# The third head group of a dilated attention: 32 by 32 score products, probabilities turned by VectorE, values re-ordered by DMA

## What is computed

```python
def dilated_window_group(q, k, v, window, dilation):
    span = window // dilation            # 128 in every group
    L = S // dilation                    # 512, 128, 32 tokens of one residue class
    # tokens are gathered by residue class mod dilation; in each class query t
    # attends the keys j <= t of its class, at most span back
    scores = einsum('bdhnqe,bdhnke->bdhnqk', qb, kw) * D ** -0.5
    m = max(scores); p = exp(scores - m); l = sum(p)
    out = einsum('bdhnqk,bdhnke->bdhnqe', p, vw) / l
    lse = m + log(l)
# the groups' outputs are weighed by softmax(lse) over the groups, then @ w_out
```

## Time and profile before

| | us |
|---|---|
| median of 3 runs (lowest, highest) | 2112.24 (2111.99, 2112.79) |
| the profiled execution, its own time | 2111.53 |
| its span, first to last instruction | 2109.7 |
| PE busy | 2098.6 |
| DVE, ACT, POOL busy | 999.5, 743.0, 1138.0 |
| attention's V1 and V2 | about 824 to 879 of the span |

### The profile page before, as it was taken

The page is one execution under the profiler, slowest core; times in us unless marked ns, Lnnn a source line. Parts: engine busy times, 40 slices in busy tenths (PEclk is TensorE's granted clock), DMA queues, the critical chain, the costliest instruction groups (busy, mean ns, idle before and its releaser), DMA issues.

```text
span 2109.7 us, 28007 instructions
## 1 busy us (share of the span) xinstructions
PE 2098.6 (99%) x11130; PEld 1743.3 (83%) x11130; DVE 999.5 (47%) x1144; ACT 743.0 (35%) x862; POOL 1138.0 (54%) x816
## 2 busy tenths in 40 slices
PE   9999999999999999999999999999999999999998
PEld 7887888888888889888888888888888888888887
DVE  6356555554123265634544332733477544543126
ACT  6334542222224455533222133514443332222234
POOL 6676465555555343375555555544566455555553
PEclk9999999999999999999999999999999999999999
DMA  5212132222232212132222222222222222223321
GB/s 198 81 61 82 41 107 92 99 99 100 100 103 106 100 60 100 60 120 100 99 99 99 100 100 100 100 99 100 84 95 99 100 100 99 98 86 106 118 100 60
DMA packets 32440, 203.34 MB, mean 96 GB/s; under 512 B 3432, under 2 KB 6248, under 8 KB 8688
## 3 DMA queue, kind: packets, MB, share of 16 engines
q1 hardware_dynamic: 32224, 202.21, 28.0%
q10 hardware_dynamic: 144, 0.09, 0.0%
HBM read 200.19 MB, written 2.10 MB: 96 GB/s over the span
## 4 chain that ended last, share of the span: by engine, by line
PE 96%; DVE 2%; ACT 1%; DMA 0%; issue 0%; SPq 0%; DVEq 0%; ACTq 0%
PE bank L1855 96%; DMA first_raw<-wall 0%; DVE x L1738 0%; PE bank L2215 0%; DVE sgate L1787 0%; DVE aqk L1561 0%; ACT w_hi L731 0%; PE bank L2117 0%; DVE h L1788 0%; DVE ssq L1812 0%; PE bank L2236 0%; DVE bank L1558 0%; DVE rot L1559 0%; ACT sgate L731 0%; SPq L569 0%
## 5 line engine op out<-in xcount | busy, mean ns | idle before, releaser
L620 POOL TENSOR_TENSOR w_lo<-raw,w_hi 128x512 fp32r<-128x512 f32 x676 | 977.6, 1476 | 863.7 <-ACT w_hi L731 863.7
L1855 PE MATMUL bank<-u_hi,w_hi 128*128 128x512 f32 (+1 forms) x1936 | 755.4, 391 | 0.1
L1855 PE MATMUL bank<-u_lo,w_hi 128*128 128x512 f32 (+1 forms) x1936 | 749.5, 387 | 0.0
L731 ACT ACTIVATE w_hi<-raw 128x2048 fp32r<-128x2048 f32 x185 | 354.3, 1915 | 930.8 <-PE bank L1855 928.0
L1855 PE MATMUL bank<-u_hi,w_lo 128*128 128x512 f32 (+1 forms) x1936 | 482.1, 387 | 0.0
L1855 PEld LDWEIGHTS bank<-u_hi,w_hi 128*128 128x128 f32 x1936 | 363.6, 188 | 75.4 <-issue 1.4
L1855 PEld LDWEIGHTS bank<-u_lo,w_hi 128*128 128x128 f32 x1936 | 363.7, 188 | 74.7 <-issue 1.4
L1855 PEld LDWEIGHTS bank<-u_hi,w_lo 128*128 128x128 f32 x1936 | 362.5, 188 | 74.7
L1855 PE MATMUL bank<-act_hi,w_hi 128*128 128x512 f32 x528 | 205.4, 389 | 0.0
L1855 PE MATMUL bank<-act_lo,w_hi 128*128 128x512 f32 x528 | 205.4, 389 | 0.0
L1270 DVE TENSOR_TENSOR h<-h,bank 128x512 f32<-128x512 f32 x48 | 30.8, 683 | 300.2 <-PE bank L1855 300.2
(11 more groups left out here) (284 smaller groups left out, 2102.5 us busy)
## 6 DMA issues: line engine op xcount, KB each, us to landing
raw<-wall SPq DMA_DIRECT2D x185, 1024.0 KB, 4.9
out_t<-h SPq DMA_DIRECT2D x8, 256.0 KB, 2.5
h<-x_t SPq DMA_DIRECT2D x3, 512.0 KB, 7.3
first_raw<-wall SPq DMA_DIRECT2D x6, 256.0 KB, 7.6
h<-x_t SPq DMA_DIRECT2D x2, 256.0 KB, 3.8
first_raw<-wall SPq DMA_DIRECT2D x4, 128.0 KB, 3.7
lmask_f<-lmask_in SPq DMA_DIRECT2D x1, 512.0 KB
cs<-cs_in SPq DMA_DIRECT2D x1, 512.0 KB, 3.4
```

The lines of the kernel that those rows point to most:

```text
L620: ins = nc.gpsimd.tensor_tensor(w_lo[:, s, c], raw[:, s, c], w_hi[:, s, c].bitcast(F32), ALU.subtract)
L731: return nc.scalar.activation(out, in_, func, **k)
L1855: return nc.tensor.matmul(out, lhsT, rhs, start=start, stop=stop, skip_group_check=True)
```

## The change

Group 2's heads are taken apart by residue mod 16. `score(hd)` makes 16 products of 32 by 32, four column groups at a time, with every fourth column of the stored queries and keys; the scores of a head are 128x128. Mask, maxima and exponentials follow that size. PE's `turn(8)` to `turn(11)` and ACT's `turned` go; DVE clears `turned_scores(hd)` (`cleared`) and writes the 32x32 squares turned onto its diagonal (`turned`, four instructions a head). For `weigh` the values must lie in the same order: after ACT's `values(2, n)` SP copies them from `av` to `av_moved[n]` in four DMAs of 32 rows each, 16 in all, before it goes on with the panel loads; `av_moved[2]` and `[3]` lie in `u_hi`, so that they wait for the last `values`. `weigh(8)` and `weigh(9)` go from n = 1 to n = 3 of the first `attn_out` panel and wait for all 16 DMAs. The eight transposes of `token_columns` take 32 rows in place of 128.

```diff
+        av_moved = [place(f"av_moved{n}", "u" if n // 2 else "a", (n % 2) if n // 2 else 42 + n, [P, S]) for n in range(TT)]
...
# SyncE
-            load_panels(PAN["a0"] + 2, PAN["down2"] + 4)
+            load_panels(PAN["a0"] + 2, PAN["attn_out"] + 2)
+            sp.wait_ge(pv_done, GH)
+            sp.wait_ge(qk_ready, 12)
+            for n in range(TT):
+                sp.wait_ge(v2_taken, n + 1 if n < 2 else TT)
+                for b in range(TT):
+                    sp.dma_start(av_moved[n][CUT * b:CUT * (b + 1), :], av[b::TT, 2, n, :]).then_inc(v_moved, 16)
+            load_panels(PAN["attn_out"] + 2, PAN["down2"] + 4)
# ScalarE
-                for n, bank in enumerate((PB[5], MS)):
-                    af(rcol[:, n * TT:(n + 1) * TT], bank[:].rearrange("p (k c) -> p k c", c=P)[:, :, 0], ACT.Copy)\
-                        .then_inc(columns_scaled, 1)
+                bank = PB[5][:, 0:2 * TT * CUT].rearrange("p (k c) -> p k c", c=CUT)
+                af(rcol[:], bank[:, :, 0], ACT.Copy).then_inc(columns_scaled, 1)
...
-                    s_n = scores_of(hd)[:, n, :]
+                    s_n = scores_of(hd)[:, n, :] if hd < 2 * GH else blocks_of(hd)[:, n * CUT:(n + 1) * CUT]
...
+                if g == 2:
+                    ins.then_inc(v2_taken, 1)
+                    if c % 2:
+                        act.wait_ge(v2_taken, c + 1)
+                        act.sem_inc(group_free, 1)
...
-            turned(8)
...
-            turned(9)
...
-            turned(10)
-            turned(11)
             conv(PAN["v2"] + 2)
# VectorE
+                if hd >= 2 * GH:
+                    ch.settle()
+                    s_h = blocks_of(hd).rearrange("p (n c) -> p n c", c=CUT)
+                    bank = score_bank(hd)[:, 0:TT * CUT].rearrange("p (n c) -> p n c", c=CUT)
+                    mask = amask[:, 2:3, 0:CUT].to_broadcast([P, TT, CUT])
...
+            def cleared(hd):
+                ch.step(nc.vector.memset(turned_scores(hd), 0.0))
+
+            def turned(hd):
+
+                dve.wait_ge(p_ready, hd + 1)
+                ch.settle()
+                for b in range(TT):
+                    rows = slice(CUT * b, CUT * (b + 1))
+                    ins = nc.vector.transpose(turned_scores(hd)[rows, :, rows], blocks_of(hd)[rows, :])
+                ins.then_inc(blocks_turned, 1)
...
             maxima(8)
             maxima(9)
+            cleared(8)
             head_sums(8)
+            turned(8)
             maxima(10)
+            cleared(9)
             head_sums(9)
+            turned(9)
             maxima(11)
+            cleared(10)
+            cleared(11)
...
             for hd in (6, 7):
                 attended(hd)
+            turned(10)
+            turned(11)
             for g in range(3):
                 dve.wait_ge(fac_upper, g + 1)
# TensorE
-                    bank, tile_of = ((PB[5], near), (MS, far))[k // TT]
-                    ins = nc.tensor.transpose(near(bank, k % TT), tile_of(rstd, k % TT), ident[:])
+                    tile_of = (near, far)[k // TT]
+                    ins = nc.tensor.transpose(PB[5][:, k * CUT:(k + 1) * CUT], tile_of(rstd[0:CUT, :], k % TT),
+                                              ident[0:CUT, 0:CUT])
...
                 for n in range(TT):
+                    if hd >= 2 * GH:
+                        for b in range(TT):
+                            ins = mm(score_bank(hd)[CUT * b:CUT * (b + 1), CUT * n:CUT * (n + 1)], near(q, n)[:, b::TT],
+                                     near(k, n)[:, b::TT])
+                        continue
...
-                pe.wait_ge(pt_ready, hd + 1)
+                if g < 2:
+                    pe.wait_ge(pt_ready, hd + 1)
+                else:
+                    pe.wait_ge(blocks_turned, hd - 2 * GH + 1)
+                    pe.wait_ge(v_moved, 16 * TT * TT)
...
-                elif (s, t) == (1, 1):
-                    turn(8)
                 elif (s, t) == (1, 2):
-                    turn(9)
                     score(10)
                     score(11)
...
                 elif (s, t) == (0, 3):
                     pe.wait_ge(lrow_ready, 3)
-                    turn(10)
-                    turn(11)
                 elif (s, t) == (1, 0):
-                    pe.wait_ge(pt_ready, AH)
                     for hd in (4, 5, 6, 7):
                         weigh(hd)
...
             def beside_first(n):
-                if n == 1:
+                if n == 3:
+                    factor(6)
+                    factor(7)
                     pe.wait_ge(group_free, GRP["attn_out"] + 2)
                     weigh(8)
                     weigh(9)
-                elif n == 3:
-                    factor(6)
-                    factor(7)
```

More of the change, by code:

```diff
@@ L363, in build @@
         pt_ready = sem("pt_ready")
+        blocks_turned = sem("blocks_turned")
+        v2_taken = sem("v2_taken")
+        v_moved = sem("v_moved")
         pv_done = sem("pv_done")
@@ L514, in by_four, with by_residue, blocks_of @@
             return t.rearrange("p (a r) -> p r a", r=TT)
-        def by_residue(t):
+        def by_residue(t, g=1):
+            if g == 2:
+                return t.rearrange("p (r b a) -> p a b r", r=TT, b=TT)
             return t.rearrange("p (r a) -> p a r", r=TT)
+        def blocks_of(hd):
+            return s_ab[hd % 2][:].rearrange("p n c -> p (n c)")[:, 0:TT * CUT]
         def by_tile(t):
@@ L1015, in attended @@
                 act.wait_ge(pv_done, hd + 1)
-                af(in_order(o_raw[:, hd, :]), by_residue(weigh_bank(hd)[:]), ACT.Copy)\
+                af(in_order(o_raw[:, hd, :], hd // GH), by_residue(weigh_bank(hd)[:], hd // GH), ACT.Copy)\
                     .then_inc(oraw_ready, 1)
@@ L1574, in maxima @@
                 r = 4 * (hd % 2)
[L1575 removed]
+                s_h = scores_of(hd)[:]
                 dve.wait_ge(s_done, hd + 1)
                 bank = score_bank(hd)[:].rearrange("p (n c) -> p n c", c=P)
[L1578 removed]
+                if hd >= 2 * GH + 2:
+                    dve.wait_ge(blocks_turned, hd - 2 * GH - 1)
+                if hd >= 2 * GH:
[4 more added lines that the diff above has]
+                else:
+                    mask = spread(0)
+                ch.step(tt(s_h, bank, mask, ALU.add))
                 if hd < GH:
@@ L1582, in maxima @@
                 ch.settle()
-                ch.step(nc.vector.tensor_reduce(mst[:, hd, :], s_h[:], AX_X, ALU.max))
+                ch.step(nc.vector.tensor_reduce(mst[:, hd, :], s_h, AX_X, ALU.max))
                 if hd < GH:
@@ L1620, in _ @@
             head_sums(7)
+            for b in range(TT):
+                rows = slice(CUT * b, CUT * (b + 1))
+                ins = cp(amask[rows, 2, 0:CUT], amask[rows, 0, rows])
+            ch.step(ins)
             maxima(8)
             maxima(9)
+            cleared(8)
             head_sums(8)
+            turned(8)
             maxima(10)
+            cleared(9)
             head_sums(9)
+            turned(9)
             maxima(11)
+            cleared(10)
+            cleared(11)
             dve.wait_ge(mrows_done, 1)
@@ L1630, in _ @@
             for g in (1, 2):
-                ch.link(tt(in_order(trow[:]), in_order(trow[:]), row_bank(g), ALU.max))
+                ch.link(tt(in_order(trow[:], g), in_order(trow[:], g), row_bank(g), ALU.max))
             for g in range(3):
-                ins = tt(in_order(erow[:, g, :]), row_bank(g), in_order(trow[:]), ALU.subtract)
+                ins = tt(in_order(erow[:, g, :], g), row_bank(g), in_order(trow[:], g), ALU.subtract)
             ins.then_inc(row_diff, 1)
@@ L1642, in _ @@
             for g in range(3):
-                tt(in_order(lrow(g)), row_bank(g), in_order(erow[:, g, :]), ALU.mult).then_inc(lrow_ready, 1)
+                tt(in_order(lrow(g), g), row_bank(g), in_order(erow[:, g, :], g), ALU.mult).then_inc(lrow_ready, 1)
             dve.wait_ge(lrow_ready, 3)
```

20 lines of the change are left out of this document (12 added, 8 removed).

## The result

| | before | after |
|---|---|---|
| median of 6 runs each, us | 2112.13 (2111.52 to 2112.79) | 2120.38 (2118.84 to 2122.24) |
| ratio of the times | | 1.0041, 95% interval 1.0031 to 1.0051 |
| profiled execution, us | 2111.5 | 2122.24 |
| its span, us | 2109.7 | 2120.4 |

The change costs 8.3 us, 0.4%; 2 us more than no change were forecast, and the range ended at 2118.2.

What follows compares the result with a forecast made beforehand. PE was taken as the bound, its chain 96% on PE. Work saved, two waits and two small terms, -3.3 + 2.5 + 2.4 + 0.2 + 0.1 = +1.9 us, gave a median of 2114.1, range 2111.0 to 2118.2.

Steps and rivals of the forecast that it cites:

- What PE loses of its work: PE's score blocks, turns and token_columns in V1 and V2: 3.3 us gained (0.7 to 4.2).
- The price of the strides: Every-fourth-column operands in the score blocks: a quarter of 1.6 us, 0.4, added to 0.9, so 1.3 for two heads.
- First wait: PE ahead of factor(0), behind DVE's eight new transposes: idle grows from 0.30 to 2.8 us, 2.5 lost (1.6 to 3.7).
- Second wait: PE ahead of weigh(8), for the last eight value DMAs on SP's queue: 2.4 us (1.6 to 4.0 likely).
- What costs nothing: cleared and the later panel load have cover; rows(mst) in V1 (1, 2) was given 0.1 us (0 to 0.5).
- Sum: All terms together: +1.9 us, 2113.4 for the profiled execution and 2114.1 for the median.
- Rival 2: TensorE's clock falls in a wait past two microseconds: one fall gives 2116.1, two 2118.1; chance 0.13.
- The price of a fall: Within the clock rival, one fall costs about 2 us, read from the run's first 20 matmuls, 0.2 apart for 4 us.
- Rival 1: Waits are small: 2111.7 in the mild form (chance 0.12), 2107.8 with both waits gone (chance 0.03).
- rival 3: Strided reads in the score blocks pay in full on both operands: +1.2 us a place, 2116.5; chance 0.06.
- rival 4: DMA between SBUF rows takes 4.9 us to landing, like a panel: second wait grows by 2.6, 2116.7; chance 0.06.

Runs made afterwards that it cites:

- e5: Changed kernel with the third group's score products reading contiguous columns (scores of other tokens) in place of every fourth; one execution of 2121.28 us.
- e3: Changed kernel with the values moved in eight DMAs of 128 KB in place of sixteen of 64 KB; 2118.86 us, ratio to before 1.0032.
- e2: Changed kernel with PE filling its two waits with 14 and 15 products whose results nobody reads; 2116.97 us, ratio to before 1.0025.
- e9: Kernel before, without the change, with twelve unread DVE transposes of 32x128 put ahead of the lower halves of the factors; 2117.4 us, ratio 1.0026.
- e1: Changed kernel with DVE turning the last two heads before it waits for the row's exponentials; 2116.95 us, ratio to before 1.0023.
- e6: Changed kernel with weigh(8), weigh(9) at n = 6 of the first output panel, weigh(10), (11) in the second, ACT's list following; 2117.62 us, ratio 1.0028.
- e7: Changed kernel with the edits of e1, e3 and e6 together; 2112.12 us, ratio to before 1.0002.
- e8: e7 with ACT's third V2 conv behind the factors' upper halves and attended(10), (11) between ACT's upper halves; 2109.08 us, ratio to before 0.9986.

## Why the prediction was wrong

By its own steps, in their order:

- **What PE loses of its work**: right in kind, 3.3 forecast, 2.8 measured. The score block is 1.47 us (1.91 less the turn's 0.44), not 1.3, so V1 (0, 3) gave 0.43 for 0.6, and V1 (1, 2) 0.83 for 1.04; V2 (0, 3) gave 1.00 for 0.99. `token_columns` gave nothing: 1.15 us from its first mark to its last before, 1.18 after.
- **The price of the strides**: 0.46 and 0.50 a block against 0.4 taken, which is luck. The 238 ns of the earlier trace rows is no price of a strided load but the mean of two kinds. In the trace of before, from 600 to 760 (contiguous columns) and from 824 to 850 (V1, every fourth column), the same group reads:

```profile
L1855 PEld LDWEIGHTS bank<-w_hi,u_lo 128*128 128x128 f32 x32 | 6.0, 188 | 1.2
...
L1855 PEld LDWEIGHTS bank<-w_hi,u_lo 128*128 128x128 f32 x27 | 8.5, 314 | 0.0
```

  So a strided load of 128 columns takes some 125 ns more and not 50. The "in full" of the prediction would have been 4.0 us a block for its 1.6, and its quarter 1.0 for its 0.4. In e5 a load of 32 columns is 110 ns long and a product 196, strided 159 and 242; of these 49 and 46 ns the block pays 7 a product (0.46 us for 64). That the four column groups side by side hide the rest was assumed, and no run shows it. On the rule of the Trainium skill (SBUF — State Buffer, section Door 1: The DMA port swizzle), that an access which crosses to a new line of 16 bytes pays, e5 agrees in sign; the rule gives no size, and paying in full is excluded.
- **First wait**: right in place and in cause, mis-sized. "I take 0.2 from start to start": it was 0.32, the upper bound being 0.35, 2.5 us for the eight; and `erow` came 0.1 and not 0.3 earlier. The wait was 3.65 where 2.8 were forecast.
- **Second wait**: right in place and in cause, mis-sized. "for 32 rows I take 0.40" a DMA on SP's queue: it was 0.59, above the bounds given (0.34 to 0.47), so the eighth was issued 4.3 us after the first, not 2.8. The landing, 2.1 us, was nearly as taken (2.3). The wait was 3.74 where 2.4 were forecast. e3 shows that the price is per DMA: half of them with twice the bytes cost 0.59 each again.
- **What costs nothing**: held. `rows(mst)` waited some 0.3 for DVE, within the bounds given. The panel load behind the sixteen DMAs held nobody.
- **Sum**: its failed step is that the clock was left at 1.00 in it, a term put at nothing. Rival 2 had named the mechanism, with the place where it decides, "from the point where a wait passes two microseconds", and the sum's own waits, 2.8 and 2.4, were past it. It was given 0.13 all the same, for "the engine was busy without pause before, and the fall at the end is one case". The runs show a fall of the granted clock at both waits, worth 3.4 us between the medians (e2) and 4.8 between the profiled spans; e9 shows that a wait alone brings one, and e2 that work in its place prevents it. With the other terms as measured the sum is -2.8 + 0.3 + 3.3 + 3.7 + 0.3 = +4.8, which is 2116.9. With the falls it is 8.2 between the medians, where 8.3 were measured, and 9.6 between the profiled executions, where 9.9 were (10.7 less the 0.8 that is not the change's). The clock is the largest miss, 3.4, next to 2.2 for the two waits and 0.5 for PE's work. Neither the clock alone (2114.1 + 3.4 = 2117.5) nor the rest alone (2116.9) would have taken the time out of the range; together they do.
- **The price of a fall**: "about 2 us" was near (1.5 for one of 3.4 us, 2.3 and 2.6 for the two of after), but it was read from the wrong place. The products at the start of the run are 0.2 us apart, yet the granted clock there reads 1.00:

```profile
2.00:4.00 2.00, 2.00 (x12) 2.00 (x11) 0.00 (x0) 0.67 (x2) 0.00 (x0) 1.00 0.84 282
```

  So their spacing shows no granted clock of 0.50, and what it comes of stays open.
- **Rivals**: two falls gave 2118.1 by rival 2, on waits that were 2.2 us too short. With those it comes to 2120.3, but two misses cancel in that: 4.0 for the falls where the medians show 3.4, and 3.3 for PE's work where it was 2.8. Rival 1 (small waits) is excluded by both waits; rival 3 (strides in full) by the block's 1.47 us and by e5; rival 4 (slow DMA) by the landing of 2.1.

The two errors of size are alike: for a new operation on a busy chain a middle between near rows was taken, where the transpose was near the upper one and the DMA's issue above both. And for what follows a long wait the case was taken in which nothing does, though the one such wait in the trace spoke for the other.

## What to carry to other kernels

Where PE is the bound and has run without a pause, price a new wait as its length plus the work at half clock behind it (3.7 us of wait cost 5.3 in e9), and where the sum's own waits are as long as an idleness after which the trace shows a fall, the fall belongs in the sum and not among the rivals. Moving data by many small DMAs costs their issues, and those behind the last producer count in full: fewer and larger DMAs and a later consumer took that wait away. A change that saves work on the bounding engine and adds stages elsewhere should be judged with the order of the other engines redone: the same change was worth +8.3 us as it was made, +0.4 with its new stages moved, and -3.0 with old ones moved too. And a mean over records of one name can hide two kinds; a price is read from the stretch that it is for.

## What the hardware showed

- Behind some waits of PE the granted clock fell to 0.50, and it stayed there for 3.4 or 6.8 us, from the windows' means:

| kernel, wait in us | fall, us after PE's last product | PE at the fall | us at 0.50 |
|---|---|---|---|
| after, 3.65 | 2.0 | idle | 6.8 |
| after, 3.74 | 2.6 | idle | 6.8 |
| e1, 3.73 | 2.0 | idle | 6.8 |
| e3, 3.65 | 2.8 | idle | 6.8 |
| e5, 3.64 | 3.0 | idle | 6.8 |
| e5, 3.72 | 3.2 | idle | 3.4 |
| e3, 2.33 | 3.0 | at work for 0.7 | 3.4 |
| e6, 1.67 | 3.2 | at work for 1.5 | 3.4 |
| e6, 3.66 | 4.6 | at work for 0.9 | 3.4 |
| e9, 3.99 | 4.8 | at work for 0.9 | 3.4 |

- The same wait of 1.66 us brought no fall in e7, and waits of 1.22 us and less brought none in any run. So the length of a wait alone doesn't say whether a fall comes, or how long it lasts; all eight waits from 3.64 us on, and the one of 2.33, had one.
- Transposes of 32x128 float32 on DVE follow one another at 0.32 us.
- A DMA between SBUF rows, 32 rows each, occupies SP's queue for 0.59 us; it lands after 2.1 us with 64 KB and 3.2 with 128 KB.
- Weight loads of 128 columns took 314 ns with every fourth column and 188 with contiguous ones; loads of 32 columns 159 and 110. Over 64 products of 32x32 only 0.46 us of it showed.
- Three DVE instructions on 4x512 with two operands (`erow`) take 1.88 us alone and 4.63 beside POOL's subtractions, 2.5 times as much. POOL loses less: its four take 5.88 there and 4.94 where DVE is idle (from 885.41 in after). DVE's RECIPROCAL on 4x512, just ahead of `erow`, took 3.34 us in after, where POOL starts halfway through it, and in e8, where POOL rests. The remedy was to move POOL's work by moving ACT's.
